# A feature-major projection by seven products of quadrants instead of eight, with its input combined one stage earlier

## The reference

```python
# end of the first block: gated branches through w_out, added to x
mixed = jnp.concatenate([y * jax.nn.silu(z) for y, z in branches], axis=-1)   # 2048 x 1280
x = x + mixed @ w_out                                                          # 2048 x 1024
# start of the second block
xn = _rms_norm(x, norm_g[l]) * (1.0 + sc_x) + sh_x
fx_in, fx_gate, qx, kx, vx, nx_gate = _split_proj(xn @ w_in[l])               # 1024 -> 3072 columns
qx = _rms_norm(_heads(qx), q_norm_g[l])                                        # norm over 64 channels
kx = _rms_norm(_heads(kx), k_norm_g[l])
```

## Time and profile before

| | |
|---|---|
| median of 3 runs | 3402.65 us (3398.95 to 3403.62) |
| profiled execution, its own time | 3402.36 us |
| its span, first to last instruction | 3400.6 us |
| mean granted TensorE clock | 0.949 |
| `tile_pass_2`, PE from first to last tile matmul | 1850.4 to 2112.2 us |
| end of `tile_pass_2` to the restart of PE behind the barrier | 2112 to 2153.3 us |
| `feature_pass_2`, PE behind the barrier | 2153.3 to 2692.9 us |

### The profile page before, as it was taken

How to read it: one execution, slowest core, us unless ns; L and a number is a source line. 1 busy time by engine, 2 the same in 40 slices (tenths; PEclk the granted TensorE clock), 3 DMA queues, 4 the chain that set the end, 5 groups by cost and what they waited for, 6 DMA issues and landing times. The chain is left out here.

```text
span 3400.6 us, 39668 instructions
## 1 busy us (share of the span) xinstructions
PE 3111.9 (92%) x14503; PEld 2445.2 (72%) x14503; DVE 1514.0 (45%) x2504; ACT 941.8 (28%) x1520; POOL 795.5 (23%) x842
## 2 busy tenths in 40 slices
PE   3799999999988999775998999899999898999899
PEld 2588887888876666553897877677888675666687
DVE  6643333042306666386455222476000145777633
ACT  4422212110112334342222234322011133555400
POOL 5322222111112222265342222011111041000111
PEclk7899999999998999778898999999999998999999
DMA  7534335122243341314102666323211235776475
GB/s 272 184 97 116 102 101 180 61 77 75 75 127 87 90 105 55 90 47 97 43 26 82 200 185 208 109 112 123 74 74 74 99 102 134 155 158 142 112 199 148
DMA packets 325559, 390.82 MB, mean 115 GB/s; under 512 B 93879, under 2 KB 260264, under 8 KB 310696
## 3 DMA queue, kind: packets, MB, share of 16 engines
q1 hardware_dynamic: 320692, 387.11, 39.9%
q10 hardware_dynamic: 4704, 1.59, 0.2%
HBM read 256.77 MB, written 135.79 MB: 115 GB/s over the span
## 5 line engine op out<-in xcount | busy, mean ns | idle before, releaser
L691 PE MATMUL f_psum_out<-f_x_high,f_w_high 128*128 128x512 f32 (+1 forms) x1472 | 573.5, 390 | 18.8 <-DVE f_x_low L668 8.1
L691 PE MATMUL f_psum_out<-f_x_low,f_w_high 128*128 128x512 f32 (+1 forms) x1472 | 569.0, 387 | 0.0
L691 PE MATMUL f_psum_out<-f_x_high,f_w_low 128*128 128x512 f32 (+1 forms) x1472 | 568.6, 386 | 0.0
L691 PEld LDWEIGHTS f_psum_out<-f_x_high,f_w_high 128*128 128x128 f32 x1472 | 279.1, 190 | 77.9 <-issue 15.0
L691 PEld LDWEIGHTS f_psum_out<-f_x_low,f_w_high 128*128 128x128 f32 x1472 | 278.9, 189 | 56.5 <-issue 1.7
L691 PEld LDWEIGHTS f_psum_out<-f_x_high,f_w_low 128*128 128x128 f32 x1472 | 278.9, 189 | 55.5
L1351 PE MATMUL nbr_psum_o<-nbr_probT,nbr_v 128*128 128x512 f32 (+3 forms) x576 | 235.8, 490 | 0.0
L683 POOL CAST f_w_high<-f_w 128x1024 fp32r<-128x1024 f32 x41 | 42.6, 1040 | 747.8 <-PE f_psum_out L691 550.5
L532 PE MATMUL p_psum_proj<-p_w_high,p_h_high 128*128 128x512 f32 x512 | 207.5, 405 | 7.4 <-issue 4.0
L532 PE MATMUL p_psum_proj<-p_w_low,p_h_high 128*128 128x512 f32 x512 | 202.1, 395 | 0.0
L532 PE MATMUL p_psum_proj<-p_w_high,p_h_low 128*128 128x512 f32 x512 | 202.1, 395 | 0.0
(11 more groups left out here) (541 smaller groups left out, 6134.0 us busy)
## 6 DMA issues: line engine op xcount, KB each, us to landing
f_w<-in_w_fm SPq DMA_DIRECT2D x45, 512.0 KB, 5.7
side_ada_w<-in_w_ada_rows SPq DMA_DIRECT2D x24, 512.0 KB, 5.7
scratch_qkmT<-p_qkT_out SPq DMA_DIRECT2D x32, 384.0 KB, 4.6
scratch_z1T<-f_out SPq DMA_DIRECT2D x10, 1024.0 KB, 4.8
p_z<-scratch_z1T SPq DMA_DIRECT2D x16, 640.0 KB, 6.6
p_xt<-in_x SPq DMA_DIRECT2D x16, 512.0 KB, 3.9
p_staging<-in_w_tok SPq DMA_DIRECT2D x8, 1024.0 KB, 8.0
scratch_hT<-p_h_slot SPq DMA_DIRECT2D x16, 512.0 KB, 3.3
```

What stands on the lines that cost most here:

```text
L691: last = nc.tensor.matmul(self.p_out[b][:, n * BANK + lo:n * BANK + hi], self.w_parts[b][w_part][:, k, :], self.x_parts[x_part][:, n, k, l ...
```

## The change

**The product.** The projection is written as a 2x2 by 2x2 product of quadrants (output block of a pair x half of the inner dimension; half of the inner dimension x even or odd token tile) and done by a scheme of seven products and sums instead of eight products. A product has 4 blocks of the inner dimension x 3 passes = 12 matmuls of 128x512. Work runs over 24 items: 2 halves of the tokens x 12 pairs of output blocks, in the order `F2_ORDER` (q/k pairs alternate with v and `f_in` pairs, then gates). Per item POOL makes four sums of weight quadrants and seven low parts, ACT seven rounded parts, DVE eight additions out of six rotating PSUM banks.

**The input.** The scratch tensor is now `x2q`, with 7 slots of 4 blocks: three plain quadrants and four combinations T1 to T4. `tile_pass_2` makes the combinations for each pair of tiles: `combine` on POOL within `tile(j, 0)`, on DVE for the last pair. `move` of a second tile stores half a slot, waits for `combined_ready`, and stores the 1024 KB of combinations. Each half of the tokens is loaded as seven pieces of 1024 KB; the second half's are loaded and split during the 12th item.

**The norms.** The sums of squares are 2 rows; they go through memory to be spread over 128 partitions as 128x16, POOL takes the root there with `pow`, and they come back broadcast through memory. The reciprocal of 128x2048 on DVE is gone.

**The border.** In the last pair the next stage's first loads stand before `tile(7, 0)` and inside `tile(7, 1)`, the last `fill` is on DVE, and six products instead of five pieces are multiplied ahead of the barrier.

```diff
+class QuadrantPass:
+    A11, A12, A22, S1, S2, S3, S4 = range(7)
+    B11, B21, B22, T1, T2, T3, T4 = range(7)
+    PRODUCTS = ((A11, B11), (S2, T2), (A12, B21), (S3, T3), (A22, T4), (S1, T1), (S4, B22))
+    N, HK, BANKS = 7, KB // 2, 6
...
+    def rest_of_x(self, eng, ops, half, i):
+        eng.wait_ge(self.x_rounded, self.N * half + i + 1)
+        ops.tensor_tensor(self.x[i][2][:], self.x[i][0][:], self.x[i][1][:], ALU.subtract).then_inc(self.x_ready[i], 1)
...
+    def product(self, pe, n, i):
+        pe.wait_ge(self.a_ready, self.N * n + i + 1)
+        if n % self.per_half == 0:
+            pe.wait_ge(self.x_ready[i], n // self.per_half + 1)
+        if self.N * n + i >= self.BANKS:
+            pe.wait_ge(self.prod_free, self.N * n + i + 1 - self.BANKS)
...
+    def combine(eng, ops, j):
+        b11, b21, b12, b22 = (slot[b][:, k:k + HK] for b in range(2) for k in (0, HK))
+        t1, t2, t3, t4 = (combined[:, n] for n in range(4))
+        eng.wait_ge(combined_stored, 16 * (j + 1))
+        ops.tensor_tensor(t1, b12, b11, ALU.subtract)
+        ops.tensor_tensor(t3, b22, b12, ALU.subtract)
+        eng.drain()
+        ops.tensor_tensor(t2, b22, t1, ALU.subtract)
+        eng.drain()
+        ops.tensor_tensor(t4, t2, b21, ALU.subtract)
+        eng.drain().then_inc(combined_ready, 1)
...
             def move(j, b):
-                i = 2 * j + b
+                i, of_pair = 2 * j + b, bass.ds(j * P, P)
                 wait_apart(sp, x_filled, i + 1, taken)
-                sp.dma_start(cols_of(d["x2T"], i), slot[b][:]).then_inc(slot_stored[b], 16)
+                if b == 0:
+                    sp.dma_start(d["x2q"][:, 0:KB, of_pair], slot[0][:]).then_inc(slot_stored[0], 16)
+                else:
+                    sp.dma_start(d["x2q"][:, KB:KB + HK, of_pair], slot[1][:, HK:]).then_inc(slot_stored[1], 16)
+                    wait_apart(sp, combined_ready, j + 1, taken)
+                    sp.dma_start(d["x2q"][:, KB + HK:, of_pair], combined[:].rearrange("p s k c -> p (s k) c"))\
+                        .then_inc(combined_stored, 16)
...
+                if b == 0 and not first:
+                    wait_apart(pool, x_filled, 2 * j, taken)
+                    combine(pool, nc.gpsimd, j - 1)
...
-                nc.vector.reciprocal(work[b][:], work[b][:])
...
+            def norm(n, b):
+                    dve.wait_ge(rms_in[b], 32 * (among(n, "qk") + 1))
...
+                if n == fp.per_half - 1:
+                    for i in range(N):
+                        fp.load_x(sp, 1, i)
```

More of the change, by code:

```diff
@@ L2175, in tile @@
                     turn_y(j + 1, b)
-                if not first:
+                if not first and not (last and b == 1):
                     turn_x(2 * j + b - 1, first=second)
@@ L2180, in _ @@
             tiles(pe, tile)
[L2181 to L2187, removed]
+            for i in range(fp.BANKS):
+                if i == 4:
+                    pe.wait_ge(x_filled, NT)
+                fp.product(pe, 0, i)
+                if i == 1:
+                    turn_x(NT - 1)
         @block.scalar
@@ L2212, in tile, with go_on @@
                     high(j + 1, b)
-                if not first:
+                if not first and not (last and b == 1):
                     fill(j + b - 1, 1 - b)
             def begin_next():
-                for b in range(2):
-                    fp.round_first_weights(nc, act, b)
-                fp.round_input(nc, act, 0, 2)
+                fp.round_x(act, 0, 0)
+                for i in range(fp.N):
+                    fp.round_w(act, 0, i)
+            def go_on():
+                fp.round_x(act, 0, 1)
+                fill(PAIRS - 1, 0)
+                fp.round_x(act, 0, 2)
+                fp.round_x(act, 0, 3)
             for k in range(MB):
@@ L2293, in tile_pass_2 @@
+            dve.wait_ge(xT_ready, NT)
+            dve.wait_ge(slot_stored[1], 16 * PAIRS)
+            dve.wait_ge(combined_stored, 16 * PAIRS)
+            for k in range(KB):
+                nc.vector.tensor_scalar(slot[1][:, k, :], p_x[:, k, :], g.scale_x[:, k:k + 1], g.shift_x[:, k:k + 1], ALU.mult, ALU.add)
+            dve.drain().then_inc(x_filled, 1)
+            dve.wait_ge(x_filled, NT)
+            combine(dve, nc.vector, PAIRS - 1)
     ph.close()
     return next_ph, fp
+F2_ORDER = (0, 4, 1, 5, 2, 6, 3, 7, 8, 9, 10, 11)
@@ L2311, in feature_pass_2 @@
[L2311 to L2315 removed]
+    HT = T // 2
+    out = [[sb(f"out{n}{b}", [P, HT]) for b in range(2)] for n in range(2)]
+    work = [sb(f"work{b}", [P, HT]) for b in range(2)]
+    high, (u2, u3) = sb("high", [P, HT], F32R), fp.u
+    spread = [sb(f"spread{b}", [P, 2 * HT // P]) for b in range(2)]
@@ new lines, in feature_pass_2, with kind_of, among @@
+    aux_free = sem("aux_free")
+    stored = [[sem(f"stored{n}{b}") for b in range(2)] for n in range(2)]
+    N = fp.N
+    QK, V, IN, GATE = (n // P // 2 for n in (2 * D2, D2, D2, 2 * D2))
+    def kind_of(j):
+        return "qk" if j < QK else "v" if j < QK + V else "in" if j < QK + V + IN else "gate"
+    items = [(half, j, kind_of(j)) for half in range(2) for j in F2_ORDER]
+    LAST = len(items) - 1
+    def among(n, *kinds):
+        return sum(kind in kinds for _, _, kind in items[:max(n, 0)])
@@ L2332, in _ @@
[L2332 to L2341, removed]
@@ L2375, in turn_v @@
-            def turn_v(j, b):
-                pe.wait_ge(vT_ready[b], j - FIRST_V + 1)
-                for n in range(NT):
-                    last = nc.tensor.transpose(fp.p_out[b][:, n * P:(n + 1) * P], row[b][:, n * P:(n + 1) * P], g.ident[:])
-                last.then_inc(v_turned[b], 1)
-            def pairs(first, end, second):
-                with pe.Fori(first, end) as j:
-                    project(j, 1, lambda: second(j, 0))
-                    project(j + 1, 0, lambda: second(j, 1))
```

462 lines of the change are left out of this document (326 added, 136 removed).

## The result

The changed kernel takes 3468.05 us in the median (3455.88 to 3471.81, 4 executions) against 3400.8 of the kernel before, a ratio of 1.0191 with a 95% interval of 1.0163 to 1.0219. It is slower by 67 us, where 3417 was forecast with 3442 as the upper end.

A forecast was written before the change was run, and what follows sets the result against it. The prediction took PE to bound the feature stage, and the tile loop to be PE-bound too but waiting for `y` every turn. 3402.4 - 60.2 + 45 + 18 + 3 + 1.5 + 8 - 0.7 = 3417 us, range 3380 to 3442.

The forecast's parts named there:

- Products, -60.2: Feature stage: 1944 matmuls behind the barrier against 2208, 264 fewer at 0.228 us, 60.2 us less.
- Combining in the loop, +45: Loop of `tile_pass_2`: SP's wait for `combine` and the larger store delay `y`, 7.5 us for each of six pairs.
- The first rival: Tile loop: the combination wait does not delay the turn, so 0 to 15 us instead of 45, 3372 to 3387; chance 0.18.
- The border, +18: Between tile loop and feature stage: later weights, pieces, splits and last combinations add 12 to 23 us, taken as 18.
- the start, +3: Behind the barrier: the first product waits for a constant's DMA (about 2) and sums and squares (about 1), 3 us.
- Norms through memory, +8: Feature stage, items after q/k ones: late factors make PE wait 0 to 2 us in each of 8 items, taken as 1.
- The third rival: Feature stage: the norm chain is longer than counted, 4 us more for each of 8 items, 3445; chance 0.12.
- Reload, +1.5: 12th item: loading and splitting the second half's seven pieces is nearly covered by PE's products, costing 1.5 us, up to 15 uncovered.
- end, -0.7: End of the feature stage: the last store is of 512 KB, 0.7 us less before the next stage.

The follow-up runs named there:

- run 1: Changed kernel with SP's wait for a pair's combinations and their store moved behind the loads of the next second tile; 3415.46 us, ratio 1.0041 to the kernel before.
- the second profile: The changed kernel itself, unaltered, run and profiled once more; median 3468.46 us, ratio 1.0202 to the kernel before, profiled execution 3470.01 us.
- the run with the split: Changed kernel with SP sending each block's sums and factors on without awaiting the other's, and POOL taking the first root earlier; 3427.73 us, ratio 1.0094.
- the one of 8181 us: Profiled execution of the changed kernel with SP's later combination store and the separate norm chains together; that kernel's median is 3374.87 us, ratio 0.9929.

## Why the prediction was wrong

- **Products, -60.2:** right. Matmuls at full clock stand 0.227 apart, and without the norms' trip the stage gives 50.6 back, where the sum without that trip has -60.2 + 1.5 + 1 = -57.7. Of the 7 us between, 3 are idle time of PE (4.3 where I had 1.5; 2.7 of it ahead of the transposes), and 2 are the sums of squares and the transposes, 38.6 us where they were 36.3; the rest is open.
- **Combining in the loop, +45:** right. +68.2 to the restart, less 21.9 of the border, are 46.3, or 7.7 a pair; of it the wait is 5.74 us (forecast 5.5) and the later landing of `y` 2.1 (forecast 2.0). The first rival (the wait is not in the ring) is refuted by run 1, which gave it all back by moving the wait and the store.
- **The border, +18, and the start, +3:** right in size (21.9 for 18 and 2). The part of it that the port makes is 5.8.
- **Norms through memory, +8:** the step that failed. Its words are "the first block's factors are back at about 26, the second's at 28" and "0 to 2 us for each of 8 items; I take 1". Counted from the item's start (2313.8 here: DVE's copy of its first product at 2316.50, less the 2.7 us of the product), the roots ended at 23.4 (forecast 22.9), but the first factors were there at 28.6. The 26 does not follow from the prediction's own numbers: two DMAs of 2.2 us behind both roots give 27.3, behind the first root alone some 24. So it lets the first factors leave before the second root is done. In SP's queue they wait for the second root and the stores of both, 3.6 us, of which their own store needs 1.4. And I gave the way back the 2.2 us of a small DMA: the two rows of a block, 4 KB each, come back as two broadcasts that write 256 KB each, four for both blocks. The first block's two had landed 4.8 us after the first was issued.
  The Trainium skill (DMA: Bandwidth & Descriptors, section Anatomy of one DMA — SWDGE (gpsimd) path) counts about 2.0 us and the bytes moved at 436 GB/s for a DMA, a fit made for another issuing path. An estimate by it is 2.6 us for one of the four and 4.4 for 1024 KB as one transfer. The trace shows more: 3.4 to 5.2 us for one, and 7.0 from the first issue to the last landing.
  From there on 15.2 us pass to DVE's copy at 43.8, where I had 13.8 (26 to 39.8). So PE, which came at 39.4, waited 5.3 us and not 0 to 2.
  The landing, in the second profile (KB of one, median us from issue to landing; with one block's two loads in a row, in the run with the split, it is 3.9):

```profile
f_work<-scratch_rms_out SPq DMA_DIRECT2D x4, 256.0 KB, 4.5
```
- **The half clock, not in the sum at all:** each gap of 3 to 5 us is followed by matmuls 0.43 apart, 15.9 to 20.8 us over the stage. A wait was priced at its own length; here it cost half as much again. With both, the norms' line is 43 to 52 instead of 8. By the second profiled execution: norms 44 more than forecast, products 7, loop and border 2, the end 1, and 3417 + 54 = 3471, where that execution took 3470.0.
- **The third rival**, the longer chain at 4 us an item and 3445, was the right one, by its idle time (4 us an item). Its price left out the clock; nor is its 3445 what the sum gives, which is 3441 with 4 us an item in place of 1 and 3449 with 4 more. Its chance of 0.12 was too low: the sum's own row had DVE at 40.6 against PE at 38.9, so the chain had no cover left, and any error in four DMAs went to PE nearly undiminished.
- **Reload, +1.5, and end, -0.7:** 1.8 us of idle in the reload item; +0.4 to +0.5 for all that follows the stage.

## What to carry to other kernels

When a DMA round trip takes the place of computation, write down its queue's program order and ask of each wait what behind it has long been ready: here two such orders cost 52 and 25 us, and changing them, and the place of one root on POOL, without removing any work turned 2% slower into 0.7% faster. Price a broadcast load by the bytes that it writes: those here, a row of 4 KB read and 256 KB written, took 3.4 to 5.2 us, where plain DMAs of 8 KB took 1.4 to 1.7 in the same item (no run varied the size). Once a chain ends at the moment its consumer needs it, nearly every us of error counts, and on PE a gap of 3 to 5 us cost its length and the half clock behind it.

## What the runs showed of the hardware

**The shared port also holds a one-input copy.** In the run without the trip, the same DVE copy stands in two norms of one item:

```profile
2290.53 0.69 DVE L2646 CAST f_high<-f_out 128x1024 fp32r<-128x1024 f32 x1
2291.32 2.14 DVE L2648 TENSOR_TENSOR f_out<-f_out,f_high 128x1024 fp32r<-128x1024 f32 x1
...
2295.77 1.62 DVE L2646 CAST f_high<-f_out 128x1024 fp32r<-128x1024 f32 x1
```

```profile
2290.80 1.57 POOL L815 TENSOR_TENSOR f_a_low<-f_sums,f_a_high 128x512 fp32r<-128x512 f32 x1 [1.42 <-ACT f_a_high L811]
2292.54 2.08 POOL L796 TENSOR_TENSOR f_sums<-f_w 128x512 f32<-128x512 f32 x1 [0.16 <-issue]
2294.56 2.27 POOL L797 TENSOR_TENSOR f_sums<-f_w 128x512 f32<-128x512 f32 x1
```

It takes 0.69 us when it starts with POOL idle and 1.62 when POOL's operation is under way, each in eight of the sixteen norms; POOL's, 1.28 alone, take 2.08 and 2.27 behind DVE's. The second copy ends 0.56 us after POOL's operation beside it (2296.83), and POOL's of 2.08 us 1.16 after DVE's (2293.46): this fits each engine waiting for the other's operation to end, in both directions.

**Equal code, unequal time.** Stages that the change does not touch ended between 1842.3 and 1854.3 us in the profiled executions of the kernels here (the one of 8181 us aside): one profiled execution per kernel carries an error of several us. A comparison by stage takes out this part, but not what one stage itself varies by, 8.4 us in the changed kernel's feature stage.
